# A product of two inputs moved from the middle of a kernel to its beginning, with its result parked in DRAM

## The reference, cut to what matters

```python
h = rms_norm(x, norm_g[l])                    # x (256, 2048)
proj = h @ w_in[l]                            # queries, keys, gates, merge logits ...
...
g_a, g_b = jnp.split(jax.nn.sigmoid(merge_logits), 2, axis=-1)
merged = g_a * (o_a @ w_up_a[l]) + g_b * (o_b @ w_up_b[l])
x = x + merged @ w_out[l]
x = x + jax.nn.sigmoid(x @ w_ple_gate[l]) * (p[l] @ w_ple[l])   # p (256, 256), w_ple (256, 2048)
```

## Time and profile before

| | |
|---|---|
| median of three runs | 2254.0 us (2253.47 to 2254.01) |
| profiled execution, span from first to last instruction | 2251.8 us |
| the profiled execution with what lies around its span, taken as the median | 2254.0 us, 2.2 more than the span |
| TensorE busy | 2225.5 us (99%), 18446 products |
| VectorE, ScalarE, PoolE busy | 1549.1, 1081.9, 414.6 us |
| mean granted TensorE clock | 0.997 |
| moved by DMA | 385.88 MB, 171 GB/s over the span |

### The profile page before, as it was taken

How to read it: one execution, slowest core, us unless ns; L and a number is a source line. 1 busy time by engine, 2 the same in 40 slices (tenths; PEclk the granted TensorE clock), 3 DMA queues, 4 the chain that set the end, 5 groups by cost and what they waited for, 6 DMA issues and landing times.

```text
span 2251.8 us, 43103 instructions
## 1 busy us (share of the span) xinstructions
PE 2225.5 (99%) x18446; PEld 2165.0 (96%) x18446; DVE 1549.1 (69%) x2611; ACT 1081.9 (48%) x1625; POOL 414.6 (18%) x327
## 2 busy tenths in 40 slices
PE   8999999999999999999999999999999999999998
PEld 7999999999999999999999988999999999999998
DVE  5556566664565567659999988899846457777564
ACT  4445554644544455344333666554545444444443
POOL 5110000000000000078878300570001001010000
PEclk9999999999999999999999999999999999999999
DMA  7766444655566665555655556566555545545652
GB/s 223 189 111 190 148 137 151 204 165 183 182 187 187 187 188 170 169 160 169 187 159 184 177 174 176 157 191 191 176 172 171 170 139 169 157 149 169 206 187 95
DMA packets 378793, 385.88 MB, mean 171 GB/s; under 512 B 14086, under 2 KB 371862, under 8 KB 378408
## 3 DMA queue, kind: packets, MB, share of 16 engines
q1 hardware_dynamic: 374394, 378.54, 55.0%
q0 software_dynamic: 2464, 3.21, 1.5%
q10 hardware_dynamic: 1744, 1.38, 0.2%
HBM read 380.72 MB, written 4.12 MB: 171 GB/s over the span
## 4 chain that ended last, share of the span: by engine, by line
PE 94%; DVE 3%; DMA 1%; ACT 1%; issue 1%; SPq 0%; POOL 0%; ACTq 0%; DVEq 0%
PE ps L449 29%; PE ps L457 28%; PE ps L453 28%; PE ps L2551 1%; DMA raw<-in_w_in_dram 1%; PE ps L2371 1%; PE ps L2600 1%; DVE wlo L401 1%; PE ps L2388 1%; PE ps L2620 1%; PE ps L2580 0%; PE ps L2407 0%; DVE op_lo L533 0%; ACT whi L394 0%; DVE ps L1797 0%
## 5 line engine op out<-in xcount | busy, mean ns | idle before, releaser
L394 ACT ACTIVATE whi<-raw 128x1024 fp32r<-128x1024 f32 (+1 forms) x688 | 722.6, 1055 | 875.6 <-PE ps L457 839.9
L401 DVE TENSOR_TENSOR wlo<-raw,whi 128x1024 fp32r<-128x1024 f32 x554 | 668.5, 1223 | 443.4 <-ACT whi L394 442.5
L449 PE MATMUL ps<-op_hi,whi 128*128 128x256 f32 (+1 forms) x5440 | 791.5, 288 | 4.5 <-DVE op_lo L1357 2.6
L453 PE MATMUL ps<-op_lo,whi 128*128 128x256 f32 (+1 forms) x5440 | 772.2, 284 | 1.1 <-DVE op_lo L1664 0.6
L457 PE MATMUL ps<-op_hi,wlo 128*128 128x256 f32 (+1 forms) x5440 | 771.2, 284 | 0.3 <-POOL wlo L401 0.3
L449 PEld LDWEIGHTS ps<-op_hi,whi 128*128 128x128 f32 x5440 | 704.2, 188 | 22.3 <-issue 12.9
L453 PEld LDWEIGHTS ps<-op_lo,whi 128*128 128x128 f32 x5440 | 706.0, 188 | 1.8 <-DVE op_lo L1664 0.8
L457 PEld LDWEIGHTS ps<-op_hi,wlo 128*128 128x128 f32 x5440 | 705.6, 188 | 0.6 <-POOL wlo L401 0.5
L401 POOL TENSOR_TENSOR wlo<-raw,whi 128x1024 fp32r<-128x1024 f32 x134 | 332.0, 2489 | 1065.0 <-ACT whi L394 1064.8
L1797 DVE SCALAR_TENSOR_TENSOR ps<-arena,param_cols,ps 128x257 f32<-128x257 f32 (+6 forms) x448 | 183.3, 488 | 0.4
L1488 DVE SCALAR_TENSOR_TENSOR arena<-arena,nslopes,ps 128x128 f32<-128x128 f32 (+1 forms) x64 | 23.7, 411 | 49.7 <-PE ps L2371 48.8
(11 more groups left out here) (383 smaller groups left out, 1437.6 us busy)
## 6 DMA issues: line engine op xcount, KB each, us to landing
raw<-in_e_w_in_dram SPq DMA_DIRECT2D x96, 1024.0 KB, 5.4
raw<-in_w_in_dram SPq DMA_DIRECT2D x84, 1024.0 KB, 5.3
raw<-in_o_w_in_dram SPq DMA_DIRECT2D x64, 1024.0 KB, 5.9
raw<-in_e_w_out_dram SPq DMA_DIRECT2D x32, 1024.0 KB, 5.7
raw<-in_w_out_dram SPq DMA_DIRECT2D x16, 1024.0 KB, 5.7
raw<-in_w_ple_gate_dram SPq DMA_DIRECT2D x16, 1024.0 KB, 5.7
raw<-in_o_w_out_dram SPq DMA_DIRECT2D x16, 1024.0 KB, 5.7
arena<-cum_rows SPq DMA_DIRECT2D x16, 544.0 KB, 6.4
```

The costliest lines, as they stand in the source:

```text
L394: nc.scalar.activation(half_view(whi[c % 2], c, n), half_view(raw[c % RING], c, n), ACT.Copy).then_inc(hi_ready, 1)
L401: own.tensor_tensor(half_view(wlo[c % 2], c, n), half_view(raw[c % RING], c, n), half_view(whi[c % 2], c, n).bitcast(F), ALU.subtract).the ...
L449: nc.tensor.matmul(o, hi8[c % 2][:, k, n * P:(n + 1) * P], MH[:, t, off:off + NT], start=(i % cpp == 0 and k == 0), stop=False)
L453: nc.tensor.matmul(o, hi8[c % 2][:, k, n * P:(n + 1) * P], ML[:, t, off:off + NT], start=False, stop=False)
```

## The change

The ple stage moves from merge's end to the front of the program. SyncE loads p and w_ple's first chunk ahead of x, and the second chunk behind x. TensorE transposes p first; pairs 0 and 1 of the product stand between the transposes of x's first and second half, pair 2 behind the filler, pairs 3 to 7 behind that, all ahead of kvc. ScalarE evicts the pairs to a new SBUF buffer `PLS` and issues two stores of 1 MB to a new internal DRAM tensor; after merge's chunk 22 SyncE reads all of it back into `PLEb`. w_ple's low halves go from VectorE to PoolE. The eight banks of PSUM are shared out anew: the pairs use banks 0 to 3, the transposed x banks 4 to 7 (only half of x at a time), so that h1 can no longer be scaled in place: it is scaled from `RES` into a new SBUF buffer `HS`, and h1's splits read `HS`. All four quarters of oa1 are split at merge's chunk 31, and upa follows merge directly. PoolE waits for both stores before its loads of cmp_w1, whose buffers lie where `PLS` was.

```diff
-            ("merge", 8, 32, 16), ("ple", 0, 2, 8), ("upa", 2, 8, 8), ...
+_STREAMS = [("ple", 0, 2, 8), ("kvc", 1, 4, 2), ... ("merge", 8, 32, 16), ("upa", 2, 8, 8), ...
-LO_ENGINE = {"kvc": "pool", ...
+LO_ENGINE = {"ple": "pool", "kvc": "pool", ...
+        HS = ar(0, DT, S1)
+        pnat = ar(4096, 2, PLE)
+        PLS = ar(6144, 16, S1)
+        ple_dram = nc.dram_tensor("ple_product", [P, 16, S1], F, kind="Internal").ap()
 # SyncE
+            nc.sync.dma_start(pnat, A["p"][0, 0]...).then_inc(S("p_landed"), 16)
+            load_ple(0)
             for part in range(4):
...
+            load_ple(1)
...
+            def ple_back(i):
+                if i == 22:
+                    sp_eng.wait_ge(S("ob_ready"), 1)
+                    sp_eng.wait_ge(S("ple_stored"), 32)
+                    nc.sync.dma_start(PLEb, ple_dram).then_inc(S("ple_back"), 16)
+            load_stream(sp_eng, "merge", between=ple_back)
 # PoolE
+            one("ple", 2)
             side("kvc")
...
+            pool.wait_ge(S("ple_stored"), 32)
             load_w1(0)
 # ScalarE
+            def ple_store(half):
+                act.wait_ge(acc_free, 4 * half + 4)
+                nc.scalar.dma_start(ple_dram[:, 8 * half:8 * half + 8, :], PLS[:, 8 * half:8 * half + 8, :]).then_inc(S("ple_stored"), 16)
+            halves(act, "act", 0)
+            square_x(0); square_x(1); x_root(0); square_x(2); square_x(3); x_root(1)
+            ple_out(0); ple_out(1); split_hi(act, 1, 0)
+            ple_out(2); split_hi(act, 1, 1)
+            ple_out(3); ple_store(0)
+            split_hi(act, 2, 0); h1_hi(0); split_hi(act, 2, 1); h1_hi(1)
+            ple_out(4); ple_out(5); h1_hi(2)
+            ple_out(6); ple_out(7); ple_store(1)
+            h1_hi(3); halves(act, "act", 3)
 # VectorE
-                    ins = V.scalar_tensor_tensor(out=o, in0=o, scalar=GC[:, t:t + 1], in1=rstd[:, 0:S1], ...)
+                    ins = V.scalar_tensor_tensor(out=HS[:, t, :], in0=RES[:, t, META:T2], scalar=GC[:, t:t + 1], in1=rstd[:, 0:S1], ...)
-                V.tensor_tensor(op(ML, S1)(g_), h1_psum(g_), op(MH, S1)(g_).bitcast(F), ALU.subtract).then_inc(ml_ready, 1)
+                split_op_dve(dve, "h1", op(HS, S1), op(MH, S1), op(ML, S1), g_)
-                    for gq in range(3):
+                    for gq in range(4):
 # TensorE
+            x_turn(0); x_turn(1)
+            pe.wait_ge(ml_ready, 1); pe.wait_ge(S("x_diag"), 1)
+            ple_pair(0); ple_pair(1)
+            x_turn(2); x_turn(3)
...
+            ple_pair(2)
+            pe.wait_ge(S("x_diag"), 4)
+            for pr in range(3, 8):
+                ple_pair(pr)
```

More of the change, by code:

```diff
@@ L65 @@
 FILL = 4
-_STREAMS = [("kvc", 1, 4, 2), ("qa", 1, 4, 2), ("qb", 1, 4, 2), ("kvs", 1, 4, 2), ("gate", 0, 1, 1), ("kvw", 1, 4, 2), ("zuz", 8, 32, 16),
-            ("merge", 8, 32, 16), ("ple", 0, 2, 8), ("upa", 2, 8, 8), ("upb", 2, 8, 8),
+_STREAMS = [("ple", 0, 2, 8), ("kvc", 1, 4, 2), ("qa", 1, 4, 2), ("qb", 1, 4, 2), ("kvs", 1, 4, 2), ("gate", 0, 1, 1), ("kvw", 1, 4, 2), ("zuz", 8, 32, 16),
+            ("merge", 8, 32, 16), ("upa", 2, 8, 8), ("upb", 2, 8, 8),
             ("out1", 4, 16, 8), ("pgate", 4, 16, 8),
@@ L585, in _ @@
                        W_in[:, :, C_GATE:C_ZA])
-            for n in ("kvw", "zuz", "merge"):
+            for n in ("kvw", "zuz"):
                 load_stream(sp_eng, n)
[L588 to L591, removed]
+            def ple_back(i):
[4 more added lines that the diff above has]
+            load_stream(sp_eng, "merge", between=ple_back)
             for n in ("upa", "upb", "out1", "pgate", "gv"):
@@ L841, in via_tmp, with square_x @@
                 return evac
-            for part in range(4):
+            def square_x(part):
                 tt, cols = part // 2, slice(1024 * (part % 2), 1024 * (part % 2) + 1024)
@@ L926, in _ @@
                 if m == 31:
-                    split_op_act(act, "p", lambda gg: pT, lambda gg: PH, 1, mg.end - 1)
-                    for j in range(3):
+                    for j in range(4):
                         split_op_act(act, "oa1", op(ZA, S1, 2), op(MH, S1, 2), 4, mg.end - 1, only=j)
@@ L931, in _ @@
                     split_hi(act, mg.c0 + 2, 1)
-                elif m < 31:
+                else:
                     halves(act, "act", mg.c0 + m + 2)
@@ L964, in _ @@
                     nc.scalar.activation(GA, GA, ACT.Sigmoid).then_inc(S("ga_sig"), 1)
[L966 to L978, removed]
             def ob1_hi(i):
                 if i < 4:
-                    split_op_act(act, "ob1", op(ZB, S1, 2), op(MH, S1, 2, 8), 4, ST["ple"].end, only=i)
+                    split_op_act(act, "ob1", op(ZB, S1, 2), op(MH, S1, 2, 8), 4, ST["merge"].end, only=i)
             side("upa", extra=ob1_hi)
@@ L1604, in merged_lo @@
                 split_op_dve(dve, "merged", op(GA, S1), op(MH, S1), op(ML, S1), gq)
-            one("ple")
-            split_op_dve(dve, "oa1", op(ZA, S1, 2), op(MH, S1, 2), op(ML, S1, 2), 3)
-            halves(dve, "dve", ST["ple"].end + 1)
             dve.wait_ge(S("ga_sig"), 1)
```

205 lines of the change are left out of this document (115 added, 90 removed).

## The result

The changed kernel takes 2257.82 us (median of 20 runs, 2255.96 to 2259.06), the kernel before beside it 2254.01 (2253.47 to 2254.72): a ratio of 1.0016, 95% interval 1.0010 to 1.0022, 3.8 us slower. The profiled execution took 2257.97, its span is 2256.2 (2251.8 before).

The account below looks back on a forecast made before the run. TensorE's queue of products bounds the kernel, transfers its beginning until 34.75 us. 12.65 + 1.2 = 13.85 us late against 12.94 saved: 0.9 slower, median 2254.9 us; range 2247.5 to 2262, the forecast's own 2251 to 2259.

Parts of the forecast that it names:

- What bounds the kernel: Whole kernel: TensorE's queue of products, 94% of the chain of waits; until 34.75 us transfers bound the beginning.
- the late gain: Merge's end and 17th chunk: ple stage 11.84, upa's pause 0.67, p's transposes 0.43, together 12.94 us off TensorE.
- the rival with 5.6 us for the read: After merge's chunk 22: PLEb's read collides with merge's loads, 5.6 us, giving 2260.5; chance 0.07.
- Transfers: Beginning: loads (6.3 us) and stores (4.9) delay kvc's chunk 2, landing 44.8, first product 45.9, 11.2 us late.
- later of the two: First product of kvc's chunk 2: the later of 45.9 (DMA) and 47.4 (engines) decides, 12.65 us late.
- the sign that was named for it: Beginning: ScalarE's wait for kvc's chunk 2 ends at about 44.8; near 40, the stores do not count.
- The chain of engines: Beginning, from x to kvc's chunk 2: 41.4 if clean, 6.7 us late; 47.4 with 6.0 us of interference, 12.65 late.
- Sharing: h1's scalings and subtractions: VectorE with two SBUF inputs and PoolE exclude each other, 6.0 us, bounds 0 and 14.2.
- the slower rival: At h1: VectorE and PoolE's six subtractions hold each other up in full, 8.0 us slower, 2262.0; chance 0.20.
- The clock: In front of kvc's chunks: TensorE's longer pause lowers the granted clock, 0 to 1.2 us, 1.2 taken.
- three nearly even chances: Whole change: faster by over 0.2% 0.25, slower by over 0.2% 0.29, within 0.46.
- The faster rival: Beginning: stores and SBUF inputs cost nothing, 41.4 decides, no clock loss, 6.2 us faster, 2247.8; chance 0.25.

Follow-up runs that it names:

- the run with the 31 rows in one piece: The mended kernel, but with the 31 rows of e_dw_w loaded in one piece as in the changed kernel: 2254.07 us.
- the mended kernel: Changed kernel with 1/rms row in PSUM, scalings before h1's subtractions, pairs 4 to 7 evicted first, four transposes, 31-row load in two: 2247.71 us.

## Why the prediction was right, and where it was off

**What bounds the kernel, and the late gain: right.** Forecast 12.94 (11.84 + 0.67 + 0.43), measured 12.99 by the shift and 13.0 in the kernel without ple work. Nothing came late in its place: upa starts without a pause, and no chunk of merge waits for a DMA; the rival with 5.6 us for the read did not occur.

**Transfers: right in size, not the bound.** The forecast landing of chunk 2, 44.8, is within what was seen with the stores (41.5 to 45.5; 45.3 and 44.6 where TensorE waited for it), 40.5 without them. It hides behind the engines here, as the forecast's "later of the two" says, so the sign that was named for it did not come: ScalarE split the chunk at 42.27, held by TensorE and not by the DMA. It decides as soon as the engines are mended. ScalarE's two store issues took 0.35 and 0.33 us, at the short end that was taken. The single engine was rightly named as the cause. The Trainium skill (DMA: Bandwidth & Descriptors, Why a DMA increments its semaphore by 16 and not by 1) gives the reason: the number of engines is the largest up to 16 that divides the outermost size, and 31 rows then get one. The traces agree: in two pieces, 16 and 15 rows, the chunk landed 7.7 us earlier.

**The chain of engines: one mechanism right, one left out; with the clock 1.9 us short** (48.6 forecast, 50.47 measured; 0.7 of the difference is the clock's). Sharing was there as described: single scalings of 2.6 us beside PoolE's, four of them, 8.6 us in all; the six that the slower rival counted did not come, since VectorE's later work met an idle PoolE. The Trainium skill (SBUF — State Buffer, Who interferes with whom) has them exclude each other for a whole instruction; the alternation one by one and its end with one input from PSUM (2624 to 482 ns at most) agree. What the step left out is the order: the chain was added up as if kvc needed only its operands, while it waited for a seventh eviction standing behind h1's third group (3.6 us of the time). Without that wait chunk 2 begins at 45.84, or about 46.7 with the changed kernel's beginning, ahead of the forecast: that the chain's number came so near is in part luck, a missing wait against a chain that was otherwise reckoned too long. The sharing itself was 8.6 us where 6.0 was taken after 3.5 us of slack, and only 1.9 us of the time went with it when it was taken away alone.

**The clock: right that it falls, 1.9 instead of 1.2**, from 37 to 42 us, behind a pause of 8.8 us. The cost does not simply follow the pause: behind 3.9 us of waiting, in the run with the 31 rows in one piece, it was 2.3 us (5.16 against 2.82).

**A term that was missing: the pace, 1.8 us.** The forecast named it as a sign of being wrong "if the products from there to merge's end are not simply shifted", and they are not. p's transposes were priced as 0.43 us to be saved, and measured so; leaving them out cost four times that, later.

Together 1.18 (15.72 - 0.69 - 13.85) + 1.8 - 0.05 of more late gain = 2.9 us, the difference between forecast and median. That the sign of the whole hung on terms of this size is what the forecast's three nearly even chances said: the sign came out as forecast, and most of the loss's size came from a wait and a pace that were not in the sum. The faster rival, 2247.8, is nearly the time of the mended kernel: its conditions had to be made first, and not all were: h1's subtractions still share, and without the load in two the same kernel takes 2254.07.

## What to carry to other kernels

Work moved to an idle stretch is priced by what stands behind it in the queues of the engines that serve it, and by the counts that the next stage waits for: a wait written for stages with two banks a pair cost more here than two engines excluding each other. Causes in parallel hide each other, so an edit worth nothing alone (the load in two) can be worth 6 us with the others: mend the one that ends last, look again, and give the kernel before the same mending before crediting the change. Where a VectorE instruction reads one input from PSUM, moving that input to SBUF was not free beside PoolE: 8.6 us on eight scalings here.

## What was not expected of the hardware

Products of 256 columns in an unbroken row start 117.5 or 118.4 ns apart at a granted clock of 1.00, for hundreds of microseconds, and something small between them can switch it: four transposes at 500 us brought the quicker pace in all six kernels that have them there (the one before, with and without the load in two, and the four runs with transposes put back), and it stayed slow until 794 us in all eight that have none. Other transposes, 16 of them at 482 us, did not switch it. What sets the pace stays open.
